# Counted lists for the first two experts, and other changes to the router of a one-core diffusion step

## Chip, core and metric

One core of a Trainium2 chip runs the whole program. The metric is the device time of one launch in microseconds (us); lower is better. The kernel before took 1672.25 us (median of 3 runs, 1671.38 to 1676.4).

## What is computed

The reference is one layer of a diffusion backbone in fp32: 1024 sample rows and 128 prompt rows of 1024 features pass a mixer with attention, an output projection with a gated residual, and then experts that choose their tokens. The part that the change touches is this:

```python
x = x + g1 * mix                                   # mix: the output projection
h = rmsnorm(x, P['norm2_g'][l]) * (1 + sc2) + sh2
# ec_ffn(h), n = 1024 sample rows (cap 128) or 128 prompt rows (cap 16)
logits = jnp.einsum('bnd,de->bne', h, w_router)
aff = jax.nn.softmax(logits, axis=-1).transpose(0, 2, 1)
gate, idx = lax.top_k(aff, cap)                    # per expert, over the rows
xs = h[idx]
hid = silu(xs @ w1) * (xs @ w3)
y = (hid @ w2) * gate                              # added back at row idx
x = x + g2 * y
```

Every one of the 16 experts takes the 128 sample rows with the highest affinity to it, and 16 prompt rows. Its three weights are 4 MB each. The order of an expert's rows is free, since each result is added back at its own row; ties go to the lower row.

## The kernel before

Rows stand in 9 tiles of 128 (8 of the sample, the last one the prompt). After the attention four things overlap, tile by tile. PE computes `out_proj(x)` (L788), x = 0 to 17, two halves of 512 features for each tile; x = 0 to 3 run inside the attention. DVE multiplies each half by the gate out of PSUM (`o_evict`, L1486). POOL adds the residual rows (L1778). ACT takes the sum of squares (L1158), the root (L1160) and the scaled rows (L1162), with two small steps on DVE between (L1493, L1499). PE then transposes the scaled rows (`h2_turn`, L812), ACT applies gain and shift out of PSUM (`h2_evict`, L1135), PE forms the logits (`logits`, L826) and, once a group of tiles is through, sums them by token (`by_token`, L834). The softmax runs in three groups, tiles 0 to 3, 4 to 7 and 8: DVE L1517 to L1519, ACT L1143, DVE L1526 to L1528. PE turns the probabilities to one row for each expert (`by_expert`, L844).

The lists are made by DVE in `pick`: for the 16 experts at once, a round takes the next 8 highest of 512 values (L1548), their indices (L1549) and strikes them out (L1551). Each sample half has 16 rounds, the prompt 2. The rounds of the first half stand between the steps of tiles 5 to 8, those of the second half come after the last output projection. Then the two sorted halves are merged: PE turns and reverses the first list (L904, L909), DVE takes the larger of each pair (L1649 to L1653), PE turns the result to columns (L913), and DVE writes `picked` and `pick_s` (L1655, L1656), which releases everything. The prompt's rows are chosen by a one-hot product on PE (L889, L896) that ACT writes out (L1168).

POOL then gathers the rows of experts 0 and 1 from HBM by an indirect DMA (L1787). PE transposes them (`gathered`, L924), DVE evicts with gain and shift (L1665), and the experts start. `expert` has 8 steps f of 32 matmuls each (L949, 16 for w1 and 16 for w3), between them the transposes of the expert before (L932), and 8 steps dm of 16 matmuls (L967), with the next expert's `gathered` between them. DVE has one product for each f (L1690), and evictions; in steps f = 2 and on, PE waits for the DVE product of two steps before. Experts 1 to 14 run in a loop of two.

The program order is written out by hand on each engine, and each engine's queue is in order. On SP, both halves of expert 0's w1 are asked for when the attention is done (L441), then the stores of rows and the next residual rows (L448 to L453), both halves of w3 after the last output projection (L457), and w2 after both first gathers have landed (L470). The layout allows that because w3 lies where the output weights lay.

## Time and profile of the kernel before

| what | us |
|---|---|
| median of 3 runs | 1672.25 |
| the profiled execution | 1671.43 |
| its span, first to last instruction | 1669.6 |
| PE, DVE, ACT, POOL busy | 1580.7, 540.6, 425.8, 110.6 |

The span and the execution's own time differ by 1.8 us, which lie outside the instructions. PE is busy for 95% of the span, and the mean granted TensorE clock is 0.980 of full speed. The page also has the span in 40 slices, the chain that ended last, and the costliest groups by line; rows are quoted below as the page and the trace's answers have them. A busy time is first to last for a merged row, and "x16" counts PE passes: an fp32 matmul is two of them, a transpose is one.

### The profile page before, as it was taken

The numbers are of one execution on the slowest core, as the hardware profiler recorded it, in microseconds if no ns is written. First come the engines' busy times: TensorE is split into PE (matmuls) and PEld (weight loads), VectorE is DVE, ScalarE is ACT, GpSimd is POOL, SyncE is SP. The second block draws the span as 40 slices with busy tenths as digits, with TensorE's granted clock in tenths as the row PEclk, the third lists the DMA queues.
The fourth block names the chain that finished last, engine by engine and source line by source line (L and its number), as shares of the span: only waits on it lengthen the run. The fifth ranks groups of instructions, "written<-read, shape, count | busy, mean of one in ns | idle before, by whom it ended". The sixth has DMA issues, their size and how long they took to land.

```text
span 1669.6 us, 26767 instructions
## 1 busy us (share of the span) xinstructions
PE 1580.7 (95%) x10877; PEld 1261.9 (76%) x10877; DVE 540.6 (32%) x1212; ACT 425.8 (26%) x982; POOL 110.6 (7%) x112
## 2 busy tenths in 40 slices
PE   4899998999999999999659999999999999999997
PEld 2745544666667667444339999999999999999996
DVE  3101333574747556116761111111111111111114
ACT  4200101454545445144411111111111111111114
POOL 0004400000000000011110000000000000000010
PEclk9999999999999999999859999999999999999998
DMA  7861003100000000143426778787777878777776
GB/s 312 313 261 49 0 0 128 37 1 14 0 0 13 0 2 1 69 183 114 151 93 248 256 275 309 260 310 263 273 266 278 304 258 316 256 276 268 282 227 240
DMA packets 113652, 288.32 MB, mean 173 GB/s; under 512 B 10112, under 2 KB 15143, under 8 KB 110399
## 3 DMA queue, kind: packets, MB, share of 16 engines
q1 hardware_dynamic: 108846, 270.27, 44.0%
q0 software_dynamic: 4752, 17.30, 3.9%
q8 instruction: 38, 0.62, 0.2%
q14 instruction: 16, 0.12, 0.0%
HBM read 265.39 MB, written 21.64 MB: 172 GB/s over the span
## 4 chain that ended last, share of the span: by engine, by line
PE 62%; issue 30%; DVE 3%; DMA 3%; POOL 1%; ACT 1%; SPq 0%; POOLq 0%; DVEq 0%; ACTq 0%
PE ps L949 30%; PE ps L967 15%; PE ps L504 8%; PE ps L566 2%; DMA wreg<-in_x_sample_dram 1%; POOL wreg L1778 1%; PE ps L517 1%; PE ps L597 1%; PE ps L924 1%; PE ps L932 1%; DMA mreg<-in_x_prompt_dram 1%; DVE list_idx L1549 1%; PE ps L557 1%; PE ps L586 1%; DVE creg L1548 1%
## 5 line engine op out<-in xcount | busy, mean ns | idle before, releaser
L949 PE MATMUL ps<-mreg,wreg 128*128 128x144 f32 x4096 | 517.5, 287 | 0.0
L949 PEld LDWEIGHTS ps<-mreg,wreg 128*128 128x128 f32 x4096 | 510.1, 190 | 0.2 <-issue 0.2
L967 PE MATMUL ps<-mreg,wreg 128*128 128x144 f32 x2048 | 265.3, 286 | 0.0
L967 PEld LDWEIGHTS ps<-mreg,wreg 128*128 128x128 f32 x2048 | 257.7, 190 | 0.0
L1690 DVE TENSOR_TENSOR mreg<-ps,mreg 128x144 f32<-128x144 f32 x128 | 39.4, 308 | 475.5 <-PE ps L949 475.5
L679 PE MATMUL ps<-wreg 128*128 128x512 f32 (+2 forms) x400 | 167.9, 519 | 0.0
L1197 ACT ACTIVATE mreg<-ps 128x144 f32<-128x144 f32 x128 | 37.3, 291 | 442.6 <-PE ps L949 442.6
L504 PE MATMUL ps<-hreg,wreg 128*128 128x512 f32 (+1 forms) x432 | 143.2, 489 | 0.0
L788 PE MATMUL ps<-wreg,mreg 128*128 128x512 f32 x288 | 128.3, 596 | 1.2 <-DVE wreg L1486 1.2
L1407 DVE TENSOR_REDUCE stat<-ps 128x1 f32<-128x1280 f32 (+1 forms) x72 | 97.7, 1358 | 90.8 <-PE ps L679 90.8
L721 PEld LDWEIGHTS ps<-const,hreg 128*128 128x128 f32 x648 | 79.9, 141 | 58.5 <-issue 38.9
L504 PEld LDWEIGHTS ps<-hreg,wreg 128*128 128x128 f32 x432 | 70.7, 191 | 70.0 <-issue 69.6
L1092 ACT ACTIVATE hreg<-ps 128x512 f32<-128x512 f32 (+2 forms) x172 | 82.2, 502 | 109.7 <-PE ps L721 107.8
L1665 DVE TENSOR_SCALAR mreg<-ps,gain,modT 128x128 f32<-128x128 f32 x128 | 52.0, 409 | 176.8 <-PE ps L924 176.8
L1104 ACT ACTIVATE hreg<-ps,stat 128x1280 f32<-128x1280 f32 (+1 forms) x72 | 88.1, 1224 | 68.3 <-DVE stat L1409 68.3
L1201 ACT ACTIVATE mreg<-ps,modT 128x128 f32<-128x128 f32 x128 | 47.0, 367 | 222.7 <-PE ps L967 222.6
L788 PEld LDWEIGHTS ps<-wreg,mreg 128*128 128x128 f32 x288 | 53.0, 190 | 61.4 <-issue 59.7
L721 PE MATMUL ps<-const,hreg 128*128 128x128 f32 x648 | 97.3, 274 | 0.0
L679 PEld LDWEIGHTS ps<-wreg 128*128 128x128 f32 x400 | 64.0, 190 | 26.9 <-issue 24.9
L736 PE MATMUL ps<-hreg,wreg 128*64 128x128 f32 x1296 | 78.5, 275 | 4.6 <-ACT hreg L1092 1.1
L736 PEld LDWEIGHTS ps<-hreg,wreg 128*64 128x64 f32 x1296 | 70.9, 137 | 13.7 <-ACT hreg L1092 9.1
L1799 POOL DMA_INDIRECT x_rows<-hreg,idx_s x15 | 23.9, 1596 | 585.3 <-DVE mreg L1665 562.0
(211 smaller groups left out, 1185.6 us busy)
## 6 DMA issues: line engine op xcount, KB each, us to landing
wreg<-in_w_e_dram SPq DMA_DIRECT2D x96, 2048.0 KB, 12.0
wreg<-in_w_ada_dram SPq DMA_DIRECT2D x24, 1024.0 KB, 10.0
out_dram<-wreg SPq DMA_DIRECT2D x9, 512.0 KB, 2.6
mreg<-in_x_sample_dram SPq DMA_DIRECT2D x8, 512.0 KB, 8.0
wreg<-in_w_out_dram SPq DMA_DIRECT2D x1, 4096.0 KB, 13.7
wreg<-in_x_sample_dram SPq DMA_DIRECT2D x8, 512.0 KB, 6.8
x_rows<-wreg SPq DMA_DIRECT2D x8, 512.0 KB, 2.8
xn_rows<-wreg SPq DMA_DIRECT2D x8, 512.0 KB, 3.7
```

Source lines behind the costliest of these rows:

```text
L504: mm = pe.matmul(bank[n % 8][:, 0:gn], w_in_sb[:, k, w_at + m * P:w_at + (m + 1) * P], hT[:, k, g0:g0 + gn], start=(k == 0), stop=(k == KD ...
L679: mm = pe.matmul(bank[3 * (n % 2) + ch][:, 0:kn], qT[:, j, t * P:(t + 1) * P], kT[:, j, k0:k0 + kn], start=True, stop=True)
L721: mm = pe.transpose(bank[MID_BANK[("turn", n, ch)]][:, a * P:(a + 1) * P], prob[n % 2][:, kt * P:(kt + 1) * P], ident)
L736: mm = pe.matmul(pv_at(t)[64 * j:64 * j + 64, :], v_sb[:, kt, 64 * j:64 * j + 64], probT[:, 2 * (t % 2) + j, src * P:(src + 1) * P], start ...
L788: mm = pe.matmul(bank[o_bank(x)], mixT[:, k, t * P:(t + 1) * P], w_out_sb[:, k, hf * 512:(hf + 1) * 512], start=(k == 0), stop=(k == KD - 1))
L949: mm = pe.matmul(o[:, 0:CAP], w[s][:, k, (f % 4) * P:(f % 4 + 1) * P], xsT[b][:, k, :], start=(k == 0), stop=(k == KD - 1))
L967: mm = pe.matmul(bank[4 + dm % 2][:, 0:CAP], w2[f // 4][:, f % 4, dm * P:(dm + 1) * P], hidT[:, f, :], start=(f == 0), stop=(f == 7))
L1092: act.activation(probT[:, 2 * (t % 2) + j, ch * 512:ch * 512 + w], bank[MID_BANK[("turn", n, ch)]][:, 0:w], ACT.Copy).then_inc(t_out, 1)
L1104: act.activation(prob[n % 2][:, 0:w], src, ACT.Exp, bias=a_neg[:, n % 4:n % 4 + 1], scale=SCALE, accum_out=a_sum[:, n % 4:n % 4 + 1]).then ...
L1201: act.activation(yT[:, dm, :], bank[4 + dm % 2][:, 0:CAPS], ACT.Copy, scale=modT[:, 0, 40 + dm:41 + dm])
L1407: dve.tensor_reduce(a_max[:, r:r + 1], src, AX_X, ALU.max).then_inc(max_ok, 1)
L1665: dve.tensor_scalar(xsT[b][:, k, 0:CAPS], bank[6 + k % 2][:, 0:CAPS], gain2[:, 0, k:k + 1], modT[:, 0, 24 + k:25 + k], ALU.mult, ALU.add). ...
```

## The change

- **Order.** The prompt tile moves from the last place to the fifth (`ORDER`); its routing (two rounds, the one-hot product's inputs) is done between the output projections. Softmax groups are now tiles 0 to 3, the prompt, 4 and 5, 6, 7.
- **Logits.** They are formed from the rows before the norm. The gain is multiplied into the router's weights once (`w_rs`, two DVE operations ahead of the first `o_evict`, beside two memsets, a copy and the reduce that was there), the row's 1/rms is applied to the logits on DVE (`by_token`, one operation for each tile in place of the copy of a group), and the shift's share of the logits comes from ten small matmuls (`shift_products`, `shift_spread`). `h2_evict` is one ACT copy of 128x512 for each half. `h2_turn` waits for POOL's add and no longer for ACT's scaled rows.
- **Last tile.** Its residual is added on DVE in two halves (`last_add`), its squares are taken in two halves.
- **Counted lists.** For experts 0 and 1 PE spreads each tile's probabilities into rows on all partitions (`spread_rows`, one transpose for each tile and expert), ACT copies them to `rank_rows`, and DVE counts for each row how many rows come before it: a `tensor_scalar` comparison with an accumulated sum, and one `scalar_tensor_tensor` for ties within the tile. The sum is the row's slot; comparing it with 0 to 127 gives a one-hot tile (`slots`), and 8 matmuls of two columns give the indices and gates (`quick_list`).
- **Full lists.** For the other experts the 16 rounds now run on both halves together (48 partitions, 512 values), inside expert 0; turning and merging stands in expert 1. The gather of expert 2 waits for them, and so do PE's transposes at the end of expert 1.
- **Weights.** First asked for are the first halves of w1 and w3; the second halves of both come once the last output projection is done. w2 waits for both first gathers as before, but the second gather now comes inside expert 0. The final norm's row is loaded after w2.
- Several semaphores are joined, and the prompt's rows are kept in place of a DMA copy (`x2_p`).

The core of the diff (the order of calls on each engine, and the counting):

```diff
+ORDER = (0, 1, 2, 3, 8, 4, 5, 6, 7)
+PLACE = {t: p for p, t in enumerate(ORDER)}
+LAST = NT - 1
+R_TILES = (range(0, 4), range(8, 9), range(4, 6), range(6, 7), range(7, 8))
+PROMPT_GROUP = 1
+QUICK = 2
...
+            first_weights(w1, w_e1, w1_in, 0)
+            first_weights(w3, w_e3, w3_in, 0)
...
-                sp.dma_start(w3[s], w_e3[0, 0, :, s * 512:(s + 1) * 512].rearrange(
-                    "(k p) f -> p k f", p=P)).then_inc(w3_in[s], 16)
-            sp.wait_ge(lg_mm, NT)
-            sp.dma_start(x2_p, x2[0]).then_inc(x2p_in, 16)
-            sp.dma_start(final_row, final_norm_g.rearrange("(a d) -> a d", a=1).to_broadcast([P, D])).then_inc(frow_in, 16)
+            first_weights(w1, w_e1, w1_in, 1)
+            first_weights(w3, w_e3, w3_in, 1)
+            sp.wait_ge(rows_in[0], 16)
+            sp.wait_ge(rows_in[1], 16)
...
             out_proj(4)
+            shift_products()
+            h2_turn(0, 0)
+            h2_turn(0, 1)
+            out_proj(5, range(0, 4))
+            shift_spread()
             logits(0)
+            out_proj(5, range(4, 6))
+            by_token(0)
+            out_proj(5, range(6, KD))
+            h2_turn(1, 0)
+            h2_turn(1, 1)
+            out_proj(6, range(0, 4))
             logits(1)
+            out_proj(6, range(4, KD))
+            by_token(1)
+            for p in range(3, 8):
+                if p > 3:
+                    out_proj(2 * p, range(0, 4))
+                    if p == 5:
+                        spread_rows(0)
+                    elif p == 6:
+                        prompt_by_expert()
+                    elif p == 7:
+                        prompt_rows()
+                    out_proj(2 * p, range(4, KD))
+                h2_turn(p - 1, 0)
+                h2_turn(p - 1, 1)
+                out_proj(2 * p + 1, range(0, 4))
+                logits(p - 1)
+                out_proj(2 * p + 1, range(4, 6))
+                by_token(p - 1)
+                out_proj(2 * p + 1, range(6, KD))
+            out_proj(16, range(0, 5))
+            spread_rows(2)
+            out_proj(16, range(5, KD))
+            h2_turn(7, 0)
+            h2_turn(7, 1)
             out_proj(17, range(0, 2))
             logits(7)
             out_proj(17, range(2, 3))
+            by_token(7)
+            out_proj(17, range(3, 5))
+            h2_turn(8, 0)
+            out_proj(17, range(5, KD))
+            spread_rows(3)
+            h2_turn(8, 1)
             logits(8)
+            prompt_features(range(0, 1))
+            by_token(8)
+            prompt_features(range(1, 4))
+            spread_rows(4)
+            prompt_features(range(4, KD))
+            quick_list(0)
+            sample_by_expert()
...
+                    if first and f == 1:
+                        quick_list(1)
+                    if lists and f in (1, 3, 5):
+                        lists[f // 2]()
+                if lists:
+                    pe.wait_ge(picks_ok, 1)
...
+            pe.wait_ge(quick_ok, 1)
+            pe.wait_ge(tok_out, NT)
...
+            for p in range(NT - 1):
+                if p in (4, 5, 7):
+                    router_exp((4, 5, 7).index(p))
+                x2_square(p)
+                if p == 4:
+                    rows_evict(0)
+                elif p == 7:
+                    rows_evict(2)
+                x2_root(p)
+                h2_evict(p, 0)
+                h2_evict(p, 1)
+                x2_scale(p)
+            last_square(0)
+            router_exp(3)
+            h2_evict(8, 0)
+            rows_evict(3)
+            last_square(1)
+            h2_evict(8, 1)
+            x2_root(8)
+            act.activation(stat[0:1, 27:28], ones[0:1, 0:1], ACT.Exp)
+            router_exp(4)
+            x2_scale(8)
+            rows_evict(4)
...
+            def above(e, t, rows, op, n):
+                width = rows.shape[1]
+                for at, piece in ((0, n), (512, n + 6)):
+                    if at < width:
+                        part = rows[:, at:min(at + 512, width)]
+                        over = passed_over()
+                        dve.tensor_scalar(over[:, 0:part.shape[1]], part, prob_e[:, t, e:e + 1], None, op, ALU.add,
+                                          accum_out=counts[:, e, t, piece:piece + 1]).then_inc(compared, 1)
...
+            def counted(g):
+                a, z = R_TILES[g][0], R_TILES[g][-1] + 1
+                dve.wait_ge(rows_out, (1, 0, 3, 5)[g])
+                for t in range(a):
+                    above(0, t, rank_rows[:, 0, a * P:z * P], ALU.is_gt, (0, 0, 3, 4)[g])
+                for t in R_TILES[g]:
+                    if t:
+                        above(0, t, rank_rows[:, 0, 0:t * P], ALU.is_ge, 1)
+                    above(0, t, rank_rows[:, 0, t * P:z * P], ALU.is_gt, 0)
+                    ties(0, t, rank_rows[:, 0, t * P:(t + 1) * P])
...
+                for t in tiles:
+                    if t:
+                        above(1, t, rank_rows[:, 1, 0:t * P], ALU.is_ge, 1)
+                    above(1, t, rank_rows[:, 1, t * P:NS], ALU.is_gt, 0)
+                    ties(1, t, rank_rows[:, 1, t * P:(t + 1) * P])
...
+            def slots(e):
+                n = NS // P
+                dve.tensor_tensor(onehot, slot_row.unsqueeze(1).to_broadcast([P, n, P]),
+                                  rank[:, e, :].unsqueeze(2).to_broadcast([P, n, P]), ALU.is_equal).then_inc(slots_ok, 1)
+            def quick_out(e):
+                dve.wait_ge(quick_mm, e + 1)
+                o = bank[QUICK_BANK[e]]
+                dve.tensor_copy(idx_g[e][:], o[:, 1:2])
+                dve.tensor_copy(pick_s[:, e:e + 1], o[:, 1:2])
+                dve.tensor_copy(picked[:, e:e + 1], o[:, 0:1]).then_inc(quick_ok, 1)
...
+            for p in range(4, 8):
+                if p == 5:
+                    normalised(0)
+                elif p == 6:
+                    normalised(1)
+                mean2(p - 1)
+                norm2(p - 1)
+                if p == 6:
+                    prompt_diagonals()
+                elif p == 7:
+                    prompt_picks()
+                o_evict(2 * p)
+                if p == 5:
+                    counted(0)
+                logits_out(p - 1)
+                by_token(p - 1)
+                if p in (4, 5, 7):
+                    shifted((4, 5, 7).index(p))
+                o_evict(2 * p + 1)
+            normalised(2)
             mean2(7)
             norm2(7)
+            counted(2)
             o_evict(16)
+            last_add(0)
             logits_out(7)
+            by_token(7)
+            shifted(3)
+            normalised(3)
+            o_evict(17)
+            last_add(1)
+            mean_last()
+            counted(3)
+            logits_out(8)
+            norm2(8)
+            by_token(8)
+            shifted(4)
+            normalised(4)
+            counted_last()
+            slots(0)
+            quick_out(0)
+            counted_second(range(0, 4))
+            probs_out(0)
             probs_out(1)
...
+            counted_second(range(4, 8))
+            slots(1)
+            at = 0
+            for f in range(8):
+                hidden(0, f)
+                if f == 1:
+                    quick_out(1)
+                n = (0, 1, 2, 1, 2, 1, 2, 1)[f]
+                sample_picks(range(at, at + n))
+                at += n
+            for dm in range(8):
+                gathered(1, dm, 8 + dm)
+                if at < CAPS // 8:
+                    sample_picks(range(at, at + 1))
+                    at += 1
+            half_lists()
+            expert(1, 1, unscattered=True, lists=(turned_lists, merged_lists, picks_out))
...
+            pool.wait_ge(quick_ok, 1)
+            rows_gathered(0)
             pool.wait_ge(xp_ok, 1)
             put_prompt(0)
             put_prompt(1)
+            pool.wait_ge(quick_ok, 2)
+            rows_gathered(1)
+            pool.wait_ge(picks_ok, 1)
```

## Rows read from the trace of the kernel before

**Rows 1.** Timeline of PE, from the last projections to the experts
```profile
813.95 1.88 PE L788 MATMUL ps<-wreg,mreg 128*128 128x512 f32 x4
...
865.36 0.66 PE L924 MATMUL ps<-const,mreg 128*128 128x128 f32 x2 [5.54 <-DMA mreg<-xn_rows,idx_g]
...
869.35 33.07 PE L949 MATMUL ps<-mreg,wreg 128*128 128x144 f32 x256
902.36 2.13 PE L967 MATMUL ps<-mreg,wreg 128*128 128x144 f32 x16
...
918.82 4.08 PE L949 MATMUL ps<-mreg,wreg 128*128 128x144 f32 x32
```

**Rows 2.** Window: PE, PEld, DVE, ACT, POOL, clock, DMA share
```profile
850.00:860.00 10.00, 1.40 (x6) 0.71 (x6) 9.10 (x28) 0.61 (x2) 0.00 (x0) 0.59 0.00 1
```

**Rows 3.** Timeline of PE among and after the output projections
```profile
701.77 13.97 PE L788 MATMUL ps<-wreg,mreg 128*128 128x512 f32 x32 [1.24 <-DVE wreg L1486]
...
724.72 0.66 PE L812 MATMUL ps<-const,wreg 128*128 128x128 f32 x4 [0.68 <-ACT hreg L1135]
...
732.85 1.04 PE L812 MATMUL ps<-const,wreg 128*128 128x128 f32 x8
...
758.37 0.96 PE L834 MATMUL ps<-quad_sum,creg 128*128 128x16 f32 x8
...
808.21 0.64 PE L826 MATMUL ps<-hreg,w_r 128*32 128x128 f32 x16 [0.43 <-DVE creg L1503]
...
840.48 2.07 PE L889 MATMUL ps<-hreg,const 16*128 16x256 f32 x4 [4.59 <-DVE hreg L1558]
843.19 6.31 PE L896 MATMUL ps<-hreg,wreg 128*128 128x256 f32 x16 [0.65 <-DVE hreg L1566]
```

**Rows 4.** Timeline of DVE: eviction, small step, softmax, one round
```profile
700.94 1.28 DVE L1486 TENSOR_TENSOR wreg<-ps,g_rows 128x512 f32<-128x512 f32 x2
...
820.33 0.15 DVE L1493 TENSOR_SCALAR stat<-stat 128x1 f32<-128x1 f32 x1 [1.68 <-ACT wreg L1158]
...
831.22 0.29 DVE L1503 COPY creg<-ps 128x128 f32<-128x128 f32 x1
...
832.72 0.68 DVE L1548 MAX8 creg<-creg 16x8 f32<-16x512 f32 x1
...
845.20 0.68 DVE L1548 MAX8 creg<-creg 16x8 f32<-16x512 f32 x1
845.92 0.08 DVE L1549 MATCH_VALUE_LOAD list_idx<-creg 16x8 f32 x1
...
846.60 0.06 DVE L1551 MATCH_VALUE_LOAD creg<-creg 16x8 f32 x1
...
847.35 0.68 DVE L1548 MAX8 creg<-creg 16x8 f32<-16x512 f32 x1
```

**Rows 5.** Groups of DVE by line and form: count, busy us, mean ns
```profile
L1407 DVE TENSOR_REDUCE stat<-ps 128x1 f32<-128x1280 f32 x64 | 95.4, 1491 | 83.1 <-PE ps L679 83.1
L1430 DVE TENSOR_SCALAR hreg<-hreg,stat 128x1280 f32<-128x1280 f32 x64 | 56.7, 886 | 2.3
```

**Rows 6.** Timeline of ACT and POOL: a tile's norm, the first gather
```profile
819.08 1.06 ACT L1158 ACTIVATE wreg<-wreg 128x1024 f32<-128x1024 f32 x1 [7.01 <-POOL wreg L1778]
820.04 0.19 ACT L1158 ACTIVATION_READ_ACCUMULATOR wreg<-wreg 128x1 f32 x1
820.25 1.28 ACT L1160 ACT_TABLE_LOAD   x1
...
860.65 1.15 POOL L1787 DMA_INDIRECT mreg<-xn_rows,idx_g  x1 [0.29 <-POOL idx_g L1785]
```

**Rows 7.** DMA issues of the page: count, KB each, median us to landing
```profile
wreg<-in_w_e_dram SPq DMA_DIRECT2D x96, 2048.0 KB, 12.0
mreg<-xn_rows,idx_g POOLq DMA_INDIRECT x16, 6.1
x_rows<-hreg,idx_s POOLq DMA_INDIRECT x15, 9.8
```

More of the change, by code:

```diff
@@ L57 @@
 RING = 6
-R_TILES = (range(0, 4), range(4, 8), range(8, 9))
+ORDER = (0, 1, 2, 3, 8, 4, 5, 6, 7)
[4 more added lines that the diff above has]
+QUICK = 2
 PICKED = T + 1124
@@ new lines, in spread_rows @@
+            def spread_rows(g):
+                pe.wait_ge(prob_ok, g + 1)
+                at = R_TILES[g][0]
+                for e in range(QUICK):
+                    if g == 2 and e == 0:
+                        pe.wait_ge(gated_ok, 1)
+                    elif g:
+                        pe.wait_ge(rows_out, (0, 0, 0, 2, 4)[g] + e + 1)
+                    for t in R_TILES[g]:
+                        mm = pe.transpose(bank[ROWS_BANK[e]][:, (t - at) * P:(t - at + 1) * P],
+                                          prob_e[:, t, e:e + 1].to_broadcast([P, P]), ident)
+                    mm.then_inc(rows_mm, 1)
@@ new lines, in quick_list, with sample_by_expert @@
+            def quick_list(e):
+                pe.wait_ge(slots_ok, e + 1)
+                pe.wait_ge(lg_out, NT)
+                for t in range(NS // P):
+                    mm = pe.matmul(bank[QUICK_BANK[e]][:, 0:2], onehot[:, t, :], prob_e[:, t, e:NE + 1:NE - e],
+                                   start=(t == 0), stop=(t == NS // P - 1))
+                mm.then_inc(quick_mm, 1)
+            def sample_by_expert():
+                pe.wait_ge(ranked, 1)
+                pe.wait_ge(rows_out, 7)
+                for t in range(NS // P):
+                    mm = pe.transpose(bank[ROWS_BANK[t // 4]][0:NE, t % 4 * P:(t % 4 + 1) * P], prob_e[:, t, 0:NE], ident)
@@ new lines, in norm2, with logits_out, by_token @@
+            def norm2(p):
+                dve.wait_ge(sqrt2_ok, p + 1)
+                dve.reciprocal(rs_x[:, p:p + 1], rs_x[:, p:p + 1]).then_inc(rec2_ok, 1)
+            def logits_out(p):
+                dve.wait_ge(lg_mm, p + 1)
+                dve.tensor_copy(lg_sb[p % 2], bank[6][:, 0:P]).then_inc(lg_out, 1)
+            def by_token(p):
+                t = ORDER[p]
+                dve.wait_ge(tok_mm, p + 1)
+                dve.wait_ge(rec2_ok, p + 1)
+                dve.scalar_tensor_tensor(out=logit[:, t, :], in0=bank[7][:, t * NE:(t + 1) * NE], scalar=rs_x[:, p:p + 1],
+                                         in1=shift_add[:, t // LAST, :], op0=ALU.mult, op1=ALU.add).then_inc(tok_out, 1)
@@ new lines, in ranks, with counted_last @@
+            def ranks(e):
+                dve.wait_ge(compared, compares[0])
+                dve.tensor_reduce(rank[:, e, :], counts[:, e, :, :], AX_X, ALU.add).then_inc(ranked, 1)
+                dve.wait_ge(ranked, e + 1)
+            def counted_last():
+                t = NS // P - 1
+                own = bank[ROWS_BANK[0]][:, 0:P]
+                dve.wait_ge(rows_mm, 7)
+                for u in range(t):
+                    above(0, u, own, ALU.is_gt, 5)
+                above(0, t, rank_rows[:, 0, 0:t * P], ALU.is_ge, 1)
+                above(0, t, own, ALU.is_gt, 0)
+                ties(0, t, own)
+                ranks(0)
@@ L1607, in _ @@
-            pick(0, range(12, 13))
+            dve.wait_ge(small_in, 16 * 9)
+            for cnd in range(2):
+                ins = dve.tensor_tensor(w_rs[:, cnd, :, :], w_r[:], gain2[:, cnd, :].unsqueeze(2).to_broadcast([P, KD, 32]),
+                                        ALU.mult)
+            dve.tensor_reduce(quad_sum[:], ident.rearrange("p (q e) -> p e q", q=4)[:, 0:NE, :], AX_X,
+                              ALU.add).then_inc(scaled_ok, 1)
+            dve.wait_ge(flip_in, 16)
+            dve.memset(counts, 0.0)
@@ new lines, in _ @@
+            dve.memset(aff[0:48, :], -1.0)
+            dve.tensor_copy(prob_e[:, 0:NS // P, NE:NE + 1], token_no.unsqueeze(2))
+            for x in range(4):
+                o_evict(x)
+            mean2(0)
+            norm2(0)
+            dve.wait_ge(add_mm, 1)
+            dve.tensor_copy(shift_rows[0:2, :], bank[7][0:2, 256:256 + NE]).then_inc(add_out, 1)
+            o_evict(4)
+            dve.wait_ge(add_mm, 2)
+            dve.tensor_copy(shift_add.rearrange("p c e -> p (c e)"), bank[7][:, 288:288 + 2 * NE]).then_inc(add_out, 1)
@@ new lines, in _ @@
+            logits_out(0)
+            mean2(1)
+            norm2(1)
+            by_token(0)
+            o_evict(5)
+            logits_out(1)
+            mean2(2)
+            norm2(2)
+            o_evict(6)
+            by_token(1)
+            logits_out(2)
+            by_token(2)
+            o_evict(7)
+            for p in range(4, 8):
[17 more added lines that the diff above has]
+                o_evict(2 * p + 1)
```

616 lines of the change are left out of this document (308 added, 308 removed).

## The prediction, made before the change was run

> **What bounds the kernel now.** The page first: PE is busy for 95% of the span, so time can only come from the stretches where it is not. The slices show one long one, at the middle of the run, and the timeline of PE dates it [rows 1]: the last output projection ends at 813.95 + 1.88 = 815.8, and expert 0's first matmul starts at 869.35. In these 53.5 us PE has only small products to do. The window of 850 to 860 [rows 2] shows who works instead: DVE is busy 9.1 of 10 us, PE 1.4, DMA nothing, and the granted clock is 0.59. DVE makes the second half's 16 rounds; one takes 847.35 - 845.20 = 2.15 [rows 4], 34 us together. Then come the gather and eight transposes: POOL issues at 860.65 [rows 6], PE has rows at 865.36, 4.7 later, and starts 4.0 after that [rows 1]. Behind 869.35 PE is dense: 33.0 for an expert's f steps, and (918.82 - 902.36)/8 = 2.06 for a dm step [rows 1]. Ahead of 815.8 PE is dense too, with three stalls of 1.24, 0.68 and 0.43 [rows 3]. So the question is what the change makes of the 53.5, and what it adds to the two dense stretches around them.
>
> **Price of a count.** No row shows a DVE comparison with an accumulated sum. The nearest is the pair of match load and index search over 512 elements, which DVE repeats at 846.60 - 845.92 = 0.68 [rows 4]; the reduce over 1280 takes 1.491 [rows 5]. Between them an element costs (1.491 - 0.68)/768 = 1.06 ns, and 0.14 is left for each operation. From below, the `tensor_scalar` L1430 has 0.886/1280 = 0.69 ns an element with everything [rows 5]. From above, the sum may be read out as on ACT, where the readout is a row of 0.19 behind the main one [rows 6]: 0.14 + 0.19 = 0.33 fixed. I take 1.06 ns and 0.14, because a count gives out one sum as the reduce does, and the pair is also two instructions. Counted from the loops: tiles 4 and 5 have 11 operations and 2816 elements, 4.5 us; tile 6 has 10 and 1792, 3.3; tile 7 has 11 and 2048, 3.7; the second expert has 15 and 4608 for each half, 7.0 and 7.0; tiles 0 to 3 have 11 and 2560, 4.3.
>
> The row of L1430 would speak for two elements a cycle. The Trainium skill, "SBUF — State Buffer", § Who interferes with whom, excepts from the two-port modes the `tensor_scalar` that also writes out its accumulator. By the row the sum below would be 5 us lower, by the rule it stands.
>
> **The stage of the output projections.** All terms against T0 = 815.8.
> - DVE has two products of 128x256, two memsets and a copy ahead of the first eviction. By 1.06 ns an element and 0.07 to 0.14 each that is 1.35. PE already waits for that eviction (the 1.24 of [rows 3]), so nothing hides it: +1.35.
> - PE gets 20 narrow passes (shift) at 0.96/8 = 0.12, 2.4; four transposes of the last tile at 1.04/8 = 0.13, 0.5; twelve spreading transposes in place of eight, 0.5, and one for the prompt, 0.1; and the prompt's rows, 2.07 at the half clock, so 1.0 here [rows 3]. Together +4.6.
> - The stalls of 0.68 (ACT's four evictions become one) and 0.43 (rounds ahead of the logits' copy) go: -1.1.
> - What is late next is DVE at the last tiles. From the end of `out_proj(15)`: PE has spread tiles 4 and 5 at 4.9, ACT copies them until 5.4, then loads the root's table, 1.28 [rows 6], and `norm2(7)` is possible at 7.1. The count takes 4.5, eviction 16, the add and the copy of the logits 1.6: 13.2. PE wants them at 11.8: +1.4. The same look at tiles 0 to 3 (count of 4.3 behind eviction 10, logits wanted at 15.0, there at 13.4) leaves no stall.
>
> POOL loses one of nine adds, and SP's queue has the same 4 MB ahead of the tiles and the same 4 MB behind the last projection, so the weights cost nothing: the second halves are wanted at f = 4, 16 us into expert 0, and land about 12 after the issue [rows 7]. T0 becomes 815.8 + 6.2 = 822.0.
>
> **From T0 to expert 0** (us behind T0).
> 1. Eviction (0.64 each, [rows 4]) and add: 1.4. ACT's half squares and readout, two small DVE steps of 0.15: 2.7.
> 2. Count of tile 6: 6.0.
> 3. Logits' copy until the softmax is handed to ACT: 832.72 - 831.22 = 1.5 [rows 4]; exponential and three steps 1.0: 8.5. PE, in order, is then in the prompt's products, 6 passes of 6.31/16 = 0.39 [rows 3], until 9.3; spread at 9.6.
> 4. Count of tile 7: 13.3. Sum of the counts and the one-hot tile (1024 elements): 14.8.
> 5. `quick_list(0)`: 16 passes at the half clock, 0.24 each, 3.8; three small copies 0.5: 19.1. The gather starts here and lands 4.7 later, or up to 9.8 later as the scatters do [rows 7], 24 to 29.
> 6. DVE meanwhile counts half of the second expert, 7.0, and copies the probabilities, 1.3: 27.4. So DVE is the last, and the gather is hidden unless it takes over 8.
> 7. Evictions of expert 0's rows, 4.0 as now: 31.4.
>
> Expert 0 starts at 822.0 + 31.4 = 853.4 in place of 869.35: -15.9.
>
> **Inside experts 0 and 1.** DVE has 7.0 + 1.5 = 8.5 before its first product; PE needs that in f = 2, after 33.0/8 x 2 = 8.3 and `quick_list(1)`, so this is covered with almost nothing to spare. `quick_list(1)` itself is 16 x 0.12 = +1.9. Ten rounds lie in the f steps: 3 rounds for two steps, 6.5 + 0.6 of 8.25, no stall. Six lie in the dm steps: 2.15 + 0.4 of DVE against PE's 2.06 in each, 0.5 x 6 less 1 of slack, +2.0. The second gather is asked for at about 12, w2 behind it at 18, there by 30, wanted at 35. Turning and merging in expert 1 is 10 narrow PE passes, +1.2. The gather of expert 2 comes at f = 5 there, 8 ahead of its use, with 6.1 as the median landing [rows 7]: 0. Together +5.1. From expert 2 on, nothing changes.
>
> **Sum.** 6.2 + 31.4 - 53.5 + 5.1 = -10.8. The profiled execution of 1671.43 would become 1660.6; its counterpart in the median is 0.8 higher: **1661.5**.
>
> **Rivals.**
> - *Counts at two elements a cycle*: tile 7's SBUF part, tiles 4 to 6 and half of the second expert shrink until PE or the gather is last: -5 more, **1656.5**. L1430 speaks for it, the reduce against. Chance 0.12.
> - *The freed time is only moved*: the count's readout costs about what ACT's does, 0.19 more on the 62 operations behind each other, +11.8, and tiles 0 to 3 then stall PE by 1.7. Or the dm steps and the second gather cost more than I have. It comes to **1672** to **1675**. For it speaks that DVE has no slack in four places above. Chance 0.18.
> - *Slower*: one mechanism, the fixed cost of a count with its semaphore. All 73 operations are then on the path; the result passes +5 us at 0.22 above my 0.14, that is from 0.36. At 0.40 it is 73 x 0.26 - 0.4 = +18.6, **1680**. No DVE row comes near; two dependent small steps of 0.15 each and a wait would. Chance 0.10.
> - *The gather is last*: it meets the 4 MB of second halves, issued some 10 behind T0 and 11 to 12 long. With the scatters' 9.8 it lands at 29, +1.6, **1663**; inside my range, and counted with the forecast.
>
> My forecast has 0.60. A measurement of this kernel tells apart about 0.3%, 5 us. Faster by more: 0.60 less a tenth for stalls that I don't see, and the 0.12, with some of the second rival's: 0.72. Within: 0.18. Slower: 0.10. The range must hold 8 in 10: down to the first rival with PE's clock kept up (-2), 1654, up to the second one, 1673.
>
> **What would show it.** Right: `out_proj` ends near 822, expert 0 begins near 853, the list's lookup product near T0 + 15, DVE busy throughout between, counts of 128x512 repeated every 0.68 and of 128x128 every 0.28, expert 0 longer by 4. Counts of 128x512 at 0.45 show the first rival, a separate row of 0.2 behind each the second. PE stalls among the output projections beyond the one at `by_token(7)`, or at expert 0's f = 2, would make the prediction too low; a DVE that waits for the gather would show the last rival.

## The result and the profile after the change

The changed kernel takes **1656.85 us** (median of 4 runs, 1656.23 to 1657.49); the kernel before took 1674.12 in the runs beside it (1671.38 to 1676.4). The ratio is 0.9898, 95% interval 0.9879 to 0.9917. The profiled execution took 1657.21, its span is 1655.2, the mean granted clock 0.989.

The page shows where. The gap at the middle of PE's slices is smaller. DVE's work around it has moved to the right, from slices 19 to 21 of the 40 into slices 21 and 22, that is, toward and into expert 0. Among the lines that the page names in the chain that ended last, the rounds (L1548, L1549, 1% of the span each) are gone, and the counts (L1714) stand with 1%. Before:

```profile
PE   4899998999999999999659999999999999999997
DVE  3101333574747556116761111111111111111114
```

After:

```profile
PE 1586.8 (96%) x10945; PEld 1265.9 (76%) x10945; DVE 551.5 (33%) x1315; ACT 416.2 (25%) x944; POOL 107.6 (7%) x109
PE   4899998999999999999879999999999999999997
DVE  3101333474746646214477111111111111111114
```

The timeline of PE answers to [rows 1] and [rows 3] (start, duration, engine, line, operation, count, and in brackets the wait and who ended it):

```profile
699.07 2.62 PE L768 MATMUL ps<-hreg,wreg 128*64 128x128 f32 x44 [0.35 <-ACT hreg L1210]
704.28 7.11 PE L821 MATMUL ps<-wreg,mreg 128*128 128x512 f32 x16 [2.60 <-DVE wreg L1635]
711.32 0.55 PE L881 MATMUL ps<-w_r,modT 128*2 128x16 f32 x16
716.26 0.61 PE L889 MATMUL ps<-creg,const 2*128 2x16 f32 x4
...
816.46 0.40 PE L873 MATMUL ps<-quad_sum,creg 128*128 128x16 f32 x2 [1.48 <-DVE creg L1661]
...
818.94 2.74 PE L821 MATMUL ps<-wreg,mreg 128*128 128x512 f32 x6
...
823.19 0.65 PE L847 MATMUL ps<-const,wreg 128*128 128x128 f32 x4 [1.29 <-DVE wreg L1643]
...
835.58 3.21 PE L937 MATMUL ps<-creg,hreg 128*128 128x2 f32 x16 [2.27 <-DVE hreg L1766]
...
846.41 0.66 PE L1013 MATMUL ps<-const,mreg 128*128 128x128 f32 x2 [5.89 <-DMA mreg<-xn_rows,idx_g]
847.82 0.80 PE L1013 MATMUL ps<-const,mreg 128*128 128x128 f32 x2 [0.76 <-DVE mreg L1894]
...
850.86 9.16 PE L1058 MATMUL ps<-mreg,wreg 128*128 128x144 f32 x64
859.86 1.84 PE L937 MATMUL ps<-creg,hreg 128*128 128x2 f32 x16
861.56 23.77 PE L1058 MATMUL ps<-mreg,wreg 128*128 128x144 f32 x192
...
885.27 2.13 PE L1082 MATMUL ps<-mreg,wreg 128*128 128x144 f32 x16
...
893.89 0.33 PE L1013 MATMUL ps<-const,mreg 128*128 128x128 f32 x1 [0.19 <-DVE mreg L1894]
...
953.85 4.08 PE L1058 MATMUL ps<-mreg,wreg 128*128 128x144 f32 x32
```

Four marks divide every run: M, the last attention product (699.07; 697.91 before); T0, the end of the last output projection (818.94 + 2.74 = 821.68); X0, expert 0's first matmul (850.86); X2, expert 2's (953.85; 967.65 before). Times from the span's start wander ahead of M: M lies at 697.1 to 701.7 in the profiled executions of the changed kernel and of the experiments. So every run is read by the stretches between the marks, which the second executions below repeat within 0.2:

| kernel | M to T0 | T0 to X0 | X0 to X2 | X2 to end | median us |
|---|---|---|---|---|---|
| before | 117.9 | 53.5 | 98.3 | 702.0 | 1674.1 |
| changed | 122.6 | 29.2 | 103.0 | 701.4 | 1656.9 |
| difference | +4.7 | -24.3 | +4.7 | -0.6 | -17.3 |

From M on the change gives 15.6 us. The profiled spans differ by 14.4, because this one was 1.2 longer ahead of M; the medians by 17.3. The kernel before lies at 1671.4 to 1676.4, and its profiled execution was one of its fastest.

The timeline of DVE answers to [rows 4]: the end of `quick_out(0)`, then counts of the second expert with their readouts, the last of the half, the copies of the probabilities, and the first eviction.

```profile
838.97 0.15 DVE L1774 COPY creg<-ps 128x1 f32<-128x1 f32 x1
839.03 0.73 DVE L1714 TENSOR_SCALAR_CACHE_REDUCE hreg<-wreg,creg 128x512 f32<-128x512 f32 x1
839.70 0.08 DVE L1714 DVE_READ_ACCUMULATOR hreg<-wreg,creg 128x1 f32 x1
839.70 0.74 DVE L1714 TENSOR_SCALAR_CACHE_REDUCE hreg<-wreg,creg 128x512 f32<-128x512 f32 x1
...
840.72 0.34 DVE L1714 TENSOR_SCALAR_CACHE_REDUCE hreg<-wreg,creg 128x128 f32<-128x128 f32 x1
...
840.99 0.73 DVE L1714 TENSOR_SCALAR_CACHE_REDUCE hreg<-wreg,creg 128x512 f32<-128x512 f32 x1
...
845.94 1.39 DVE L1780 COPY creg<-ps 16x512 f32<-16x512 f32 x2
847.36 0.73 DVE L1894 TENSOR_SCALAR mreg<-ps,gain,modT 128x128 f32<-128x128 f32 x2
```

A count of 512 repeats after 839.70 - 839.03 = 0.67, one of 128 after 840.99 - 840.72 = 0.27. That is 0.40/384 = 1.04 ns an element and 0.14 fixed; the readout has a row of its own, but the next count starts beside it.

### The profile page after: what moved, and what is told of

Its sections match the earlier page's. It is cut to its first block, busy times and chain, and to the rows that moved or that the text cites. A ratio compares the mean times of both kernels' runs of the same rounds, so it can differ in the third digit from the quotient of the medians.

```text
span 1655.2 us, 26952 instructions
## 1 busy us (share of the span) xinstructions
PE 1586.8 (96%) x10945; PEld 1265.9 (76%) x10945; DVE 551.5 (33%) x1315; ACT 416.2 (25%) x944; POOL 107.6 (7%) x109
## 4 chain that ended last, share of the span: by engine, by line
PE 94%; DVE 3%; DMA 1%; ACT 1%; issue 1%; SPq 0%; DVEq 0%
PE ps L1058 30%; PE ps L1082 15%; PE ps L711 9%; PE ps L537 9%; PE ps L821 7%; PE ps L768 5%; PE ps L753 4%; PE ps L681 3%; PE ps L598 2%; PE ps L694 1%; PE ps L722 1%; PE ps L550 1%; DVE hreg L1714 1%; PE ps L629 1%; PE ps L1013 1%; PE ps L1021 1%
## 5 line engine op out<-in xcount | busy, mean ns | idle before, releaser
L1577 DVE TENSOR_SCALAR hreg<-hreg,stat 128x1280 f32<-128x1280 f32 (+1 forms) x72 | 59.0, 820 | 2.5
## 6 DMA issues: line engine op xcount, KB each, us to landing
wreg<-in_w_out_dram SPq DMA_DIRECT2D x1, 4096.0 KB, 13.4
```

Of the source, the lines that this page charges most:

```text
L1577: dve.tensor_scalar(prob[n % 2][:, 0:w], prob[n % 2][:, 0:w], a_rec[:, r:r + 1], None, ALU.mult).then_inc(norm_ok, 1)
```

## The experiments

Times in microseconds; unless said, each stands against the changed kernel, by the marks.

**The change a second time**, and the kernel before a second time.

> The changed kernel once more, as the measure for the others beside it. Theory (the 16 rounds of the second half left the path, counting took their place, 7 us of other work came in around it): 14 us below the kernel before, as its profiled executions stand apart (1671.4 and 1657.2). Rival (the medians' 17 us are what the change is worth): 17 us below again. Expert 0 starts at 850.9, the last output projection ends at 821.7.

> The kernel before once more, for a second profile. In the changed kernel's profiles the start of the last attention product differs by up to 4.6 us from run to run (699.1 to 701.7), with a longer stretch at the low clock between 40 and 60 us. Theory: the same wandering lies in the kernel before, and its first profile was an early one; from the last attention product to the end it takes 971.7 us again, whatever the total. Rival: the part behind the attention differs too, which would make 14 or 17 us a matter of the change.

Measured: the changed kernel 1657.34, ratio 0.9899 (0.9882 to 0.9917); its stretches are 122.6, 29.2, 102.9 and 701.3. The kernel before, one execution, 1671.65: 118.1, 53.4, 98.3 and 701.9. The medians are 17.5 apart again, as the first text's rival had it and not its theory. From M on the kernel before takes 971.8, as the second text's theory had it, and the changed kernel 956.1 both times, so 15.6 to 15.7 of the difference lie there. M moved by 2.0 (699.07, 697.10) between the two executions of the changed kernel; the 4.6 in the second text is the distance of 697.1 to 701.7, not of the 699.1 that it names. The differences that follow are read on this, with one reserve: later runs show that the clock alone, with the same work, can shift T0 to X0 by 1.0 and the last stretch by 0.7. A smaller difference there, from one profile, has to be looked for in the rows.

**Before's order of the weight halves.** Both halves of w1 are asked for after the attention, both of w3 after the last projection.

```diff
-            first_weights(w3, w_e3, w3_in, 0)
+            first_weights(w1, w_e1, w1_in, 1)
...
-            first_weights(w1, w_e1, w1_in, 1)
+            first_weights(w3, w_e3, w3_in, 0)
             first_weights(w3, w_e3, w3_in, 1)
...
```

The edit also gives the weights the places in SBUF that they had before.

> The changed kernel with expert 0's weights asked for as before: both halves of w1 ahead of the tiles, both halves of w3 behind the last output projection. Theory: nothing (within 1 us of the changed kernel), since 4 MB stand at each place in both orders and the late ones land some 12 us before expert 0 starts. Rival (the order of halves is part of the gain): expert 0 would wait for w3's first half at its start, if that lands after 850.9, and the time rises by 1 to 5 us.

Measured: 1656.76, ratio 0.9895 (0.9876 to 0.9915), all four stretches within 0.1. The theory holds: the new order of the weight halves is worth nothing here.

**Rounds back on the path.** The 16 rounds run ahead of expert 0's evictions, and not inside its steps.

```diff
             counted_second(range(0, 4))
...
+            sample_picks(range(CAPS // 8))
             for k in range(KD):
                 gathered(0, k, k)
...
```

> The changed kernel with all 16 rounds back ahead of expert 0's rows on DVE. Theory: one round is 2.15 us, 16 are 34.4; expert 0 starts that much later, 885.3, and gets 1.7 back because its dm steps no longer wait for DVE: 32 to 34 us slower, 1690. Rival (the gain comes from the order of tiles and the logits before the norm, and the rounds would be hidden anyway by the gather and the half-speed clock): under 10 us slower.

Measured: 1691.26, ratio 1.0102 (1.0078 to 1.0126), slower than before the change. T0 to X0 is 62.3, +33.1; X0 to X2 gives 1.0 back: the dm steps take 16.5 again (-1.7), while expert 0's f steps take 0.8 longer. From M on that is 32.6, as the theory had it. PE's timeline has it in one wait:

```profile
881.75 0.79 PE L1013 MATMUL ps<-const,mreg 128*128 128x128 f32 x2 [34.25 <-DVE mreg L1895]
```

The gain is the rounds' leaving the path; the counts are what makes that possible, and cost part of it: with the rounds back, T0 to X0 is 62.3 against 53.5 before the change. No run takes out the new order of tiles or the logits before the norm alone, so what each of these is worth is not shown.

**The count behind the evictions.** The first half of the second expert's count runs after expert 0's rows are evicted.

```diff
             quick_out(0)
-            counted_second(range(0, 4))
...
             for k in range(KD):
                 gathered(0, k, k)
+            counted_second(range(0, 4))
             counted_second(range(4, 8))
```

> The changed kernel with the first half of the second expert's count (15 operations, 6.9 us) moved behind the evictions of expert 0's rows. Theory (the gather is almost as late as DVE): expert 0 starts when the gather has landed, only about 1 us sooner (849.9), then PE waits for the second expert's list behind f = 1 for 6 us: 5 to 6 us slower. Rival (DVE alone sets the start): expert 0 starts 6.9 sooner, 844, the wait gives it back, 0 in sum.

Measured: 1666.76, ratio 0.9958 (0.9943 to 0.9973), 9.2 slower from M on where the theory had 5 to 6. T0 to X0 is 28.3, 0.9 sooner; X0 to X2 is 113.8, +10.8. The timeline of PE:

```profile
852.60 9.99 PE L1058 MATMUL ps<-mreg,wreg 128*128 128x144 f32 x64
867.98 3.58 PE L937 MATMUL ps<-creg,hreg 128*128 128x2 f32 x16 [5.40 <-DVE hreg L1766]
```

The wait is 5.4. The passes behind it are slow too: the same 16 passes took 1.84 in the changed kernel, and the next 192 passes took 26.49 in place of 23.77. So a wait of 5.4 costs 5.4 + 1.7 + 2.7, and the 0.8 more in the first 64 passes brings the sum to 10.6 of the 10.8. The theory had the wait nearly right (6) and left the clock out. Windows of PE (busy, granted clock, DMA share, GB/s) show it fall with the wait and recover some 10 later:

```profile
860.00:865.00 5.00, 2.59 (x22) 1.00 0.01 2
865.00:870.00 5.00, 2.02 (x10) 0.67 0.00 0
870.00:875.00 5.00, 5.00 (x23) 0.50 0.23 39
875.00:880.00 5.00, 5.00 (x35) 0.80 0.59 191
880.00:885.00 5.00, 5.00 (x43) 1.00 1.02 412
```

**The multiplies away from POOL's additions.** This looks at a surprise: `normalised` (L1693), one small product, took 0.17 in some groups and over 2 in others.

```diff
             for p in range(4, 8):
-                if p == 5:
-                    normalised(0)
-                elif p == 6:
-                    normalised(1)
                 mean2(p - 1)
...
                     shifted((4, 5, 7).index(p))
+                    normalised((4, 5, 7).index(p))
                 o_evict(2 * p + 1)
-            normalised(2)
```

> The changed kernel with the last softmax steps of three groups ahead of the eviction that releases POOL's add, not behind it. In the changed kernel their last product (128x64, 128x16, 128x32) takes 2.13 to 2.15 us in place of the 0.23 of the kernel before, and each time it starts with POOL's add of 2.34 us. Theory (DVE is held by POOL's add while both read two tiles): the three products take about 0.2, and the time does not change by 1 us, since no wait ends on them. Rival (the product is slow for another reason, its operands' place): it stays at 2.1.

Measured: 1658.41, ratio 0.9906 (0.9889 to 0.9923). As the theory had it, the three multiplies took 0.23, 0.17 and 0.19. DVE in the changed kernel, POOL in the same, and DVE in this one:

```profile
755.44 2.13 DVE L1693 TENSOR_TENSOR creg<-creg 128x64 f32<-128x64 f32 x1
755.14 2.34 POOL L2065 TENSOR_TENSOR hreg<-hreg 128x1024 f32<-128x1024 f32 x1 [13.27 <-DVE hreg L1635]
```
```profile
756.44 0.23 DVE L1693 TENSOR_TENSOR creg<-creg 128x64 f32<-128x64 f32 x1
```

Nothing came of it on the path: M to T0 stays at 122.6. T0 to X0 was 1.0 shorter and X0 to X2 0.8 longer, a pattern of the clock (below).

**ACT copies expert 0's probabilities.**

```diff
-            probs_out(0)
-            probs_out(1)
...
+            act.wait_ge(back_mm, 2)
+            for half in range(2):
+                act.activation(aff[32 * half:32 * half + NE, :], bank[ROWS_BANK[half]][0:NE, :], ACT.Copy).then_inc(aff_out, 1)
...
```

> The changed kernel with the two copies of the probabilities (16x512, 1.39 us on DVE ahead of expert 0's evictions) done by ACT, which is idle there. Theory: DVE is free at 845.9, the gather lands at 846.4 and becomes the last, so expert 0 starts about 1 us sooner, not 1.4. Rival (the evictions wait for the gather already): 0.

Measured: 1656.89, ratio 0.9907 (0.9891 to 0.9924). T0 to X0 is 28.7, 0.5 shorter, half of what the theory had: DVE was free 1.4 earlier and then waited 0.8 for the transposes of the gathered rows, which landed at 845.17. The clock fell early here as in the changed kernel (the list's 16 passes took 3.22 and 3.21), so the 0.5 is the edit's.

**The rounds spread.** Two of the six rounds stay in expert 0's dm steps, four go to the first steps of expert 1, and the turning moves back.

```diff
-                if at < CAPS // 8:
+                if dm < 2:
...
+            expert(1, 1, unscattered=True, lists={0: rest, 1: rest_lists, 3: turned_lists, 4: merged_lists, 5: picks_out})
...
```

> The changed kernel with four of the six rounds of expert 0's dm steps moved into steps f = 0 and 1 of expert 1, and the lists' turning and merging in its steps 3, 4, 5 in place of 1, 3, 5. Theory (DVE needs 2.55 us for a round and an eviction where PE needs 2.06): the eight dm steps of expert 0 take 16.5 us again in place of 18.2, expert 1 takes as long as now, so 1.5 us faster. Rival (the steps are long for another reason, such as the DMA traffic that starts there): they stay at 18.2.

Measured: 1656.36, ratio 0.9902 (0.9886 to 0.9919). The eight dm steps take 902.48 - 885.52 = 17.0 in place of 18.2 (the theory had 16.5), with one stall of 0.19 left; expert 1's steps are unchanged. From M to the end only 0.6 of the 1.2 shows: T0 to X0 is 0.7 shorter and expert 0's f steps are 0.65 longer, the same pattern of the clock, and the last stretch is 701.9 in place of 701.4.

**The head into the attention.** The reduce, two memsets and the copy move from DVE's head of the output projections into the last block of attention.

```diff
                     scaled(n + 1)
+                    if not more and n == 6:
+                        dve.wait_ge(proj_mm, 48)
+                        dve.wait_ge(flip_in, 16)
+                        dve.tensor_reduce(quad_sum[:], ident.rearrange("p (q e) -> p e q", q=4)[:, 0:NE, :], AX_X, ALU.add)
+                        dve.memset(counts, 0.0)
...
```

> The changed kernel, with the reduction for quad_sum, the two memsets and the copy of the token numbers moved from VectorE's head of the output projections into the last block of attention, where VectorE has free time between the products of two tiles. My theory: these stand on the path, because TensorE waits 2.60 us at the head of the output projections (1.24 in the kernel before) for VectorE, and 0.9 us of VectorE's head are these instructions. The wait becomes 1.6 to 1.8 us, and the time from the last attention product to the end of the span falls from the changed kernel's 956.1 to 955.1 to 955.4. Rival: the saved time only becomes a longer wait for the first o_evict or last_add of the stage (the wait of 1.48 us at the turning of tile 7 grows), then the span does not change and expert 0 begins at the same distance from the last attention product.

Measured: 1657.28, ratio 0.9904 (0.9887 to 0.992). The wait at the head is 1.75. M to the end of the span is 955.1, as my theory had it, and yet the theory is mostly wrong: T0 is only 0.25 sooner. PE starts the stage 0.84 sooner, and its timeline shows who took the rest: behind a new wait at `by_token(0)` only 0.38 is left, and behind a longer one at `by_token(7)`, 1.60 for 1.48, 0.25. The rival, which had the wait at tile 7 growing, is so partly right.

```profile
717.65 0.40 PE L873 MATMUL ps<-quad_sum,creg 128*128 128x16 f32 x2 [0.20 <-DVE creg L1668]
815.14 0.40 PE L873 MATMUL ps<-quad_sum,creg 128*128 128x16 f32 x2 [1.60 <-DVE creg L1668]
```

The other 0.7 lies at the end, X2 to end 700.6 in place of 701.4, and the runs with the count behind the evictions, with the early multiplies and with ACT's copies have it too. It lies in the last transposes, which run at a lower clock in one execution than in another: 0.66 in the window of 1640 to 1645 of the changed kernel, 1.00 in that of 1638 to 1643 with ACT's copies. The same row in the changed kernel, then with ACT's copies:

```profile
1642.72 0.63 PE L1107 MATMUL ps<-const,hreg 128*128 128x128 f32 x2
```
```profile
1640.82 0.38 PE L1107 MATMUL ps<-const,hreg 128*128 128x128 f32 x2
```

**Late halves.** The second halves of expert 0's two weights are asked for behind its gathered rows.

```diff
             sp.wait_ge(o_mm, 2 * NT)
-            first_weights(w1, w_e1, w1_in, 1)
-            first_weights(w3, w_e3, w3_in, 1)
...
             sp.wait_ge(rows_in[0], 16)
+            first_weights(w1, w_e1, w1_in, 1)
+            first_weights(w3, w_e3, w3_in, 1)
```

> The changed kernel, with the second halves of expert 0's two weights asked for only once its gathered rows have landed, so that the gather has the DMA engines to itself. My theory: the gather, which took 6.3 us from issue to landing beside these halves and 4.6 us in the kernel before, comes back to 4.6 to 5.2 us, but VectorE is free for the rows only at 847.3, 0.9 us after they were there, so that expert 0 begins as soon after the last output projection as in the changed kernel (28.2 to 29.2 us), and the last product to end of span stays at 956.1 within 0.4. Rival: the place of the halves matters, either as a gain (the gather ends last, 1 to 1.7 us sooner) or as a loss (expert 0's later matmuls wait for the halves, which now land some 10 us after the rows: a wait of 1 us or more on TensorE at the first column that reads a second half).

Measured: 1656.83, ratio 0.9899 (0.9882 to 0.9915). Expert 0's gather took 4.3 in place of 6.3, and T0 to X0 stays at 29.2, as the theory had it: PE had rows at 843.32 and then waited for DVE. In all runs with the late halves it took 4.3 to 4.5, in those profiled beside the halves 5.8 to 7.0. No later matmul waits for a half.

```profile
843.32 0.66 PE L1013 MATMUL ps<-const,mreg 128*128 128x128 f32 x2 [3.95 <-DMA mreg<-xn_rows,idx_g]
846.67 0.79 PE L1013 MATMUL ps<-const,mreg 128*128 128x128 f32 x2 [2.70 <-DVE mreg L1894]
```

**The last five together.** Each of the five edits from the multiplies on, as above.

> The changed kernel with five edits together: the multiplies of the running sum away from POOL's additions, expert 0's probabilities copied out by ScalarE, the rounds of the second list spread as in the run before, the head moved into attention, and the late halves. My theory: the single effects add up, as each stands in another place of the path: 0.9 (multiplies) + 0.9 (head) + 1.0 (probabilities; more where the gather then ends last and is now sooner) + 0.7 (rounds), so that the last attention product to the end of the span takes 952.0 to 953.5 instead of 956.1, and the ratio to the kernel before is 0.987 to 0.9885. Rival: TensorE's path from the last output projection to expert 0's rows is set by the clock that it is granted there, and a shorter wait gives the time back in slower matmuls: 954.5 or more.

Measured: 1655.11, ratio 0.9891 (0.9874 to 0.9907). M to the end is 951.3: T0 0.3 sooner, T0 to X0 26.8 (-2.4), X0 to X2 101.6 (-1.4), the end -0.8. That is below the theory's 952.0 to 953.5, while the ratio by time, 0.9891, is above its 0.987 to 0.9885; and its 0.9 for the multiplies was the clock's. T0 to X0 gained more than the single edits add up to, so two of them ran by themselves.

**ACT's copies with the late halves.** These two edits alone.

> The changed kernel with two of the earlier edits together: expert 0's probabilities copied out by ScalarE, and the second halves of its weights asked for behind its rows. Alone the first brought expert 0's first matmul 0.5 us nearer to the last output projection (28.7 instead of 29.2) and the second nothing (29.2), and in the kernel with all edits the same stretch took 26.8, less than the single effects add up to. My theory: VectorE's copies and the gather end within a microsecond of each other, so each edit alone only uncovers the other wait; together they give the whole 1.4 us of the two copies, so the stretch takes 27.7 to 27.9 and TensorE's transposes wait for VectorE and not for the gather. Rival: the excess came from the other edits of that kernel (the multiplies taken away from POOL's additions, and a clock that fell later there), and the stretch takes 28.4 to 28.8 as with the first edit alone.

Measured: 1655.13, ratio 0.989 (0.9872 to 0.9908). T0 to X0 is 26.8 again, 847.70 - 820.87, X0 to X2 102.8. Alone the two gave 0.5 and 0; so the excess needs neither the multiplies nor the other edits, and the rival (28.4 to 28.8) is out. DVE is last again, not the gather:

```profile
834.61 2.44 PE L937 MATMUL ps<-creg,hreg 128*128 128x2 f32 x16 [3.49 <-DVE hreg L1769]
842.93 0.66 PE L1013 MATMUL ps<-const,mreg 128*128 128x128 f32 x2 [4.15 <-DMA mreg<-xn_rows,idx_g]
844.66 0.80 PE L1013 MATMUL ps<-const,mreg 128*128 128x128 f32 x2 [1.08 <-DVE mreg L1895]
847.70 8.98 PE L1058 MATMUL ps<-mreg,wreg 128*128 128x144 f32 x64
```

The gain is 1.0 more than my theory's 1.4, and the list's 16 passes show most of it: 2.44 here, 3.21 in the changed kernel. Windows of the changed kernel, then of this one (PE, PEld, DVE, ACT, POOL busy with counts, granted clock, DMA share, GB/s):

```profile
825.00:830.00 5.00, 2.82 (x11) 1.70 (x12) 3.88 (x24) 3.58 (x6) 0.00 (x0) 0.92 0.05 20
830.00:835.00 5.00, 3.31 (x10) 2.43 (x9) 4.65 (x24) 4.06 (x10) 0.00 (x0) 0.74 0.81 248
835.00:840.00 5.00, 4.42 (x23) 3.97 (x24) 1.70 (x7) 0.00 (x0) 0.00 (x0) 0.60 1.05 398
```
```profile
825.00:830.00 5.00, 2.83 (x14) 2.25 (x15) 3.75 (x23) 3.50 (x7) 0.00 (x0) 1.00 0.00 0
830.00:835.00 5.00, 1.51 (x10) 1.03 (x8) 4.49 (x20) 3.35 (x8) 0.00 (x0) 1.00 0.26 105
835.00:840.00 5.00, 3.78 (x22) 2.83 (x22) 2.91 (x14) 1.16 (x2) 1.65 (x3) 0.59 0.00 0
```

The clock first fell ahead of 830 in one and behind 835 in the other. Both patterns occur with the same work there: the late halves alone had the early fall, and the early multiplies, with the changed kernel's work behind T0, the late one. Against that run, where DVE did the copies and T0 to X0 was 28.2, the gain is the 1.4 of the copies. This kernel and the one with five edits are the best measured; the marks set them 2.5 and 4.0 ahead of the changed kernel at X2, of which about 1.0 is the clock's, while the intervals of the ratios overlap, so the gain by time alone isn't settled.

## Why the prediction was right, and where its sizes were off

The sign, the mechanism and the order of the steps were right: 1661.5 was forecast, 1656.85 came, inside the range, and 4.7 below the forecast. By the steps, each against the marks:

- **Price of a count.** 1.06 ns and 0.14 were forecast, 1.04 and 0.14 measured. Tile 6 took 827.43 - 824.22 = 3.2 (3.3), tile 7 3.65 (3.7), half of the second expert 845.94 - 839.03 = 6.9 (7.0). This settles the rivals on price. The first one had counts of 512 repeat at 0.45; they repeat at 0.67. The time alone would not have told: that rival's 1656.5 is nearer to the measured 1656.85 than my 1661.5. The "freed time only moved" and the "slower" rival both need a higher fixed cost: the readout row exists, 0.08, but lies beside the next count. The other branch of the former, dearer dm steps or a late second gather, did not come either: the dm steps cost 1.7, and no wait ends on that gather. One number of that rival was also wrong as worked out: 13.4 + 11 x 0.19 = 15.5 against 15.0 makes a stall of 0.5 at tiles 0 to 3, not 1.7. The Trainium skill's exception for the accumulating `tensor_scalar` ("SBUF — State Buffer", § Who interferes with whom) agrees with the 0.67 for 512 elements.
- **Stage of the output projections:** +6.2 forecast, +4.7 measured. The head was right: the wait grew by 2.60 - 1.24 = 1.36 (1.35). So was the wait at `by_token(7)`, 1.48 (1.4). Too large was the term for the shift: 20 narrow passes took 0.55 + 0.61 = 1.16, not 2.4, and 16 of them follow each other every 0.03. They have only two columns on the stationary side (128*2 in the row). The forecast priced them all by a row of `by_token`, whose passes move the same 16 columns but have 128 on the stationary side; that this makes the difference is read from these two shapes, not tested. I did not foresee the wait of 1.29 at 823.19 for the last add; it lies behind T0, where DVE sets the pace.
- **T0 to expert 0:** 31.4 forecast, 29.2 measured. Against the list of the seven steps, in us behind T0:

| end of | forecast | measured |
|---|---|---|
| the norm's small steps | 2.7 | 2.5 |
| count of tile 6 | 6.0 | 5.75 |
| spread of tile 7 | 9.6 | 8.6 |
| count of tile 7 | 13.3 | 12.25 |
| one-hot tile | 14.8 | 13.9 |
| list and three copies | 19.1 | 17.35 |
| gather (24 to 29) | | 24.7 |
| half count and copies | 27.4 | 25.65 |
| evictions | 31.4 | 29.2 |

  Two steps hold most of it. The spread came 1.0 sooner, 0.25 of it from the steps before; the six prompt passes ahead of it, priced at 0.39 each by the half clock, took 0.30 each (1.77 from 828.01), and the window of 825 to 830 has a granted clock of 0.92. And the list's passes, forecast at the half clock, ran at a mixed one, 3.2 + 0.25 for 4.3. The transposes and evictions took 3.5 for 4.0. That DVE and not the gather is last was right, by 0.9.
- **Inside experts 0 and 1:** +5.1 forecast, +4.7 measured. `quick_list(1)` took 1.84 (1.9), but expert 0's f steps grew only by 34.4 - 33.0 = 1.4, since the matmuls around it took 0.3 less than before. The dm steps took 903.45 - 885.27 = 18.2 for 16.5 (+1.7, forecast 2.0) with four stalls of 0.19 for DVE's evictions, expert 1's steps +1.6 (1.2). Expert 0 is so longer by 3.1, where the signs had 4. The list in f = 2 was covered, as said; the run with the count behind the evictions shows what its lack costs. (The matmuls that the text ahead of the prediction counts in these steps, 32 and 16, are PE passes.)
- **From expert 2 on** nothing changes: -0.6, about the size of what the clock in the last 15 us makes.
- **The gather is last:** it landed 6.3 behind its issue beside the weights' halves and was not last, but by less than a microsecond. That is why two edits that gave 0.5 and nothing alone gave the full 1.4 together, once the clock's 1.0 is taken off.
- **The weights cost nothing:** the run with before's order shows it for the order of the halves, and the late halves for their place behind the gather.
- **The signs** came, but for one: DVE is not busy throughout from T0 to X0. It waits 3.3 for the list's passes, which the forecast has as a step of PE.

The forecast's difference of 10.8 missed 4.8 of the 15.6: 1.5 in the stage, 2.2 in the tail, 0.4 in the experts, 0.6 at the end. All have one sign. Two choices of price hold most of it: the shift's passes by a row of another shape, and the half clock throughout the tail. The remaining 1.7 between 15.6 and the medians' 17.3 isn't located: of the kernel before only two of its faster executions (1671.43 and 1671.65) were profiled.

## What to carry to other kernels

When a stretch is bound by serial work on one engine, ask which result the next stage needs first and compute only that, even by a costlier method: here 73 operations that count, for two experts, let the 16 rounds for the others run beside the matmuls. If two waits end within a microsecond of each other, test the edits for both together, since each alone may show little (here 0.5 and 0, and 1.4 together). Compare executions between marks in the trace and not by their spans: an edit here hit its expected span to 0.1 us and owed most of that to the clock in the last rows.

## What the runs showed of the hardware that was not expected

- A DVE product with two inputs in SBUF took 2.13 at 755.44 beside a POOL addition of 2.34 that began 0.3 earlier, and ended with it; moved away from it, 0.23. The Trainium skill, "SBUF — State Buffer", § Who interferes with whom, says that a DVE instruction with two SBUF inputs contends with a GpSimd (POOL) instruction that reads SBUF; the traces agree, with a factor of nine.
- The counts show as TENSOR_SCALAR_CACHE_REDUCE with a readout row of 0.08, beside which the next count already runs.
- With the same work the granted clock fell from 1.00 ahead of 830 in some executions and behind 835 in others (windows above), worth 1.0 at expert 0's start. In four of the kernels where it fell late (rounds back on the path, count behind the evictions, early multiplies, rounds spread), expert 0's first 64 passes then took 9.80 to 9.99 for 9.16 and gave most of it back; in the two best kernels they took 8.98 and 9.02. What decides it was not found.
- Behind a wait of 5.4 on PE inside expert 0 the passes took 4.4 longer, at a granted clock of 0.50 and 0.80 in the two windows from 870 to 880.
